# A decoder layer on one core: the output norm's reciprocal root as exponential of minus half a logarithm on ScalarE

## What is computed

```python
D_MODEL, SEQ = 1024, 256
def rms_norm(x, g):
    y = x * lax.rsqrt(jnp.mean(x * x, axis=-1, keepdims=True) + 1e-6)
    return y * g
...
h = rms_norm(x, norm_pre_g)
proj = h @ w_in                       # q, k, v, gate of both groups, forget logits
y_a = merge_heads(fox_attention(q_a, k_a, v_a, log_f)) * silu(g_a)
y_b = merge_heads(moba_attention(q_b, k_b, v_b, slopes)) * silu(g_b)
y = concatenate([y_a, y_b]) @ w_out
return x + rms_norm(y, norm_post_g)   # this last norm is what the change touches
```

## Time and profile before

| | |
|---|---|
| median of 3 runs | 152.05 us (150.95 to 152.28) |
| profiled execution, its own time | 150.72 us |
| span of its instructions | 148.9 us |
| TensorE busy | 140.1 us (94%) |
| VectorE, ScalarE, GpSimd busy | 114.1, 97.4, 53.2 us |
| mean granted TensorE clock | 0.993 of full speed |

### The profile page before, as it was taken

The page is one execution under the profiler, slowest core; times in us unless marked ns, Lnnn a source line. Parts: engine busy times, 40 slices in busy tenths (PEclk is TensorE's granted clock), DMA queues, the critical chain, the costliest instruction groups (busy, mean ns, idle before and its releaser), DMA issues.

```text
span 148.9 us, 2929 instructions
## 1 busy us (share of the span) xinstructions
PE 140.1 (94%) x1012; PEld 131.1 (88%) x1012; DVE 114.1 (77%) x241; ACT 97.4 (65%) x200; POOL 53.2 (36%) x76
## 2 busy tenths in 40 slices
PE   7899999999999999999999979999999999999930
PEld 7898999999999999999999879899999778898830
DVE  0486956999999996879798897989979796222591
ACT  5467889299954687794995729667676765234340
POOL 5641100000000260077390963919184664120421
PEclk9999999999999999999999999999999999999997
DMA  3899997679676998848654624446460440000034
GB/s 99 241 322 399 399 394 274 226 267 292 259 230 263 405 340 319 258 181 228 178 167 145 211 50 158 151 145 211 141 205 6 150 203 0 0 4 0 0 141 141
DMA packets 13948, 29.05 MB, mean 195 GB/s; under 512 B 1512, under 2 KB 6640, under 8 KB 13680
## 3 DMA queue, kind: packets, MB, share of 16 engines
q1 hardware_dynamic: 13344, 27.66, 54.8%
q10 hardware_dynamic: 592, 1.22, 2.1%
HBM read 25.73 MB, written 1.06 MB: 180 GB/s over the span
## 4 chain that ended last, share of the span: by engine, by line
PE 67%; issue 12%; POOL 11%; DMA 2%; ACT 2%; DVE 2%; POOLq 1%; SPq 0%; DVEq 0%
PE bank L843 30%; PE bank L853 16%; PE bank L1001 11%; POOL bias L321 4%; PE bank L954 4%; POOL probs L338 3%; POOL xg_lo L344 2%; DMA raw<-in_w_units 2%; ACT probs L482 1%; PE bank L935 1%; PE bank L937 1%; PE bank L936 1%; PE bank L943 1%; POOL x_t L373 1%; PE bank L945 1%
## 5 line engine op out<-in xcount | busy, mean ns | idle before, releaser
L574 DVE TENSOR_TENSOR w_lo<-raw,w_hi 128x1024 fp32r<-128x1024 f32 (+1 forms) x34 | 48.3, 1425 | 5.2 <-ACT w_hi L387 5.0
L387 ACT ACTIVATE w_hi<-raw 128x1024 fp32r<-128x1024 f32 (+1 forms) x34 | 35.7, 1060 | 6.8 <-PE bank L843 2.8
L843 PE MATMUL bank<-h_lo,w_hi 128*128 128x256 f32 x128 | 35.6, 278 | 0.0
L843 PE MATMUL bank<-h_hi,w_hi 128*128 128x256 f32 x128 | 35.6, 278 | 0.0
L843 PE MATMUL bank<-h_hi,w_lo 128*128 128x256 f32 x128 | 35.6, 278 | 0.0
L321 POOL TENSOR_TENSOR bias<-squares,causal 128x256 f32<-128x256 f32 (+1 forms) x8 | 12.5, 1587 | 35.1 <-DMA squares<-decay_rows_scratch 35.1
L338 POOL TENSOR_TENSOR probs<-probs,row_inv 128x256 f32<-128x256 f32 (+1 forms) x16 | 12.9, 827 | 33.7 <-DVE row_inv L716 33.7
L843 PEld LDWEIGHTS bank<-h_hi,w_hi 128*128 128x128 f32 x128 | 24.1, 188 | 0.5
L843 PEld LDWEIGHTS bank<-h_lo,w_hi 128*128 128x128 f32 x128 | 24.0, 188 | 0.5
L843 PEld LDWEIGHTS bank<-h_hi,w_lo 128*128 128x128 f32 x128 | 24.0, 188 | 0.0
L482 ACT ACTIVATE probs<-logits,neg_max 128x128 f32<-128x128 f32 (+1 forms) x32 | 14.2, 445 | 12.4 <-DVE neg_max L710 12.4
(11 more groups left out here) (123 smaller groups left out, 311.2 us busy)
## 6 DMA issues: line engine op xcount, KB each, us to landing
raw<-in_w_units SPq DMA_DIRECT2D x30, 512.0 KB, 5.5
raw_out<-in_w_out SPq DMA_DIRECT2D x4, 512.0 KB, 6.6
v_pair<-v SPq DMA_DIRECT2D x8, 256.0 KB, 4.1
raw<-in_w_out SPq DMA_DIRECT2D x4, 512.0 KB, 3.5
h<-in_x SPq DMA_DIRECT2D x2, 512.0 KB, 7.6
squares<-decay_rows_scratch ACTq DMA_DIRECT2D x1, 1024.0 KB, 5.7
x_t<-in_x SPq DMA_DIRECT2D x1, 1024.0 KB, 5.1
raw<-in_w_units SPq DMA_DIRECT2D x3, 256.0 KB, 4.7
```

What stands on the lines that cost most here:

```text
L387: nc.scalar.activation(w[0][:, s, 0:width], raw[:, s, 0:width], ACT.Copy).then_inc(s_hi, 1)
L574: nc.vector.tensor_tensor(w[1][:, s, 0:width], raw[:, s, 0:width], w[0][:, s, 0:width].bitcast(F32), ALU.subtract).then_inc(s_lo, 1)
L843: last = nc.tensor.matmul(dst, stationary(a, j), moving(b, j), start=n == 1, stop=n == count * len(PASSES))
```

## The change

For each row tile ScalarE computes rstd itself. VectorE adds up only the groups before the last one, with EPS: that is `ms` now, a partial mean square. ScalarE takes Ln of (last group's sum / 1024 + partial mean square), the partial mean square being the activation's bias, and then Exp of minus half of it, which is `rstd`. The one-element Sqrt ahead of the loop, both roots, the reciprocals and the Newton steps are gone. VectorE multiplies group 1 by the gains right behind group 0's sum, waits for row tile 0's `rstd` behind group 2's product, and adds up groups 2 and 3 ahead of the products of groups 3 and 4.

```diff
--- before.py
+++ after.py
@@ -543,14 +543,16 @@
             probs_high(PAIRS - 1)
             y_high(PAIRS - 1)
 
-            nc.scalar.activation(junk[:, 0, 0:1], rstd[:, 0:1], ACT.Sqrt).then_inc(s_table, 1)
-            act.wait_ge(s_table, 2)
             for n, (t, cols, group) in enumerate(out_groups):
                 act.wait_ge(s_group, n + 1)
                 nc.scalar.activation(junk[:, t, cols], group, ACT.Square, accum_out=out_sq[:, n:n + 1]).then_inc(s_osq, 1)
                 if cols.stop == D_MODEL:
                     act.wait_ge(s_oms, t + 1)
-                    nc.scalar.activation(root[:, t:t + 1], ms[:, t:t + 1], ACT.Sqrt).then_inc(s_oroot, 1)
+                    act.wait_ge(s_osq, n + 1)
+                    nc.scalar.activation(root[:, t:t + 1], out_sq[:, n:n + 1], ACT.Ln, bias=ms[:, t:t + 1],
+                                         scale=1.0 / D_MODEL).then_inc(s_oroot, 1)
+                    act.wait_ge(s_oroot, t + 1)
+                    nc.scalar.activation(rstd[:, t:t + 1], root[:, t:t + 1], ACT.Exp, scale=-0.5).then_inc(s_rstd, 1)
             act.wait_ge(s_ypost, len(out_groups))
             act.wait_ge(s_rstd, TT + 1)
             nc.scalar.activation(y_post[:, 1, HALF + SEQ:], y_post[:, 1, HALF + SEQ:], ACT.Copy,
@@ -791,8 +793,8 @@
                 kept = group if n == 3 else y_post[:, t, cols]
                 nc.vector.tensor_tensor(kept, group, gpost_row[:, cols], ALU.mult).then_inc(s_ypost, 1)
 
-            def out_rstd(t, groups):
-                r, a, m = newton[:, 0, t:t + 1], newton[:, 1, t:t + 1], ms[:, t:t + 1]
+            def out_partial(t, groups):
+                m = ms[:, t:t + 1]
                 for n in groups:
                     dve.wait_ge(s_osq, n + 1)
                     if n == groups[0]:
@@ -803,15 +805,6 @@
                     if n != groups[-1]:
                         link(ins)
                 ins.then_inc(s_oms, 1)
-                times_g(groups[-1])
-                dve.wait_ge(s_oms, t + 1)
-                link(nc.vector.tensor_scalar(a, m, -0.5, None, ALU.mult))
-                dve.wait_ge(s_oroot, t + 1)
-                link(nc.vector.reciprocal(r, root[:, t:t + 1]))
-                link(nc.vector.scalar_tensor_tensor(out=a, in0=r, scalar=a, in1=r, op0=ALU.mult, op1=ALU.mult))
-                nc.vector.scalar_tensor_tensor(out=rstd[:, t:t + 1], in0=a, scalar=1.5, in1=r, op0=ALU.add,
-                                               op1=ALU.mult).then_inc(s_rstd, 1)
-                dve.wait_ge(s_rstd, t + 2)
 
             def residual(t, c, groups):
                 dve.wait_ge(s_ypost, groups)
@@ -821,11 +814,15 @@
                                                in1=x_nat[:, t, cols], op0=ALU.mult, op1=ALU.add).then_inc(s_fin[t][c], 1)
 
             times_g(0)
-            out_rstd(0, (0, 1))
+            out_partial(0, (0,))
+            times_g(1)
             times_g(2)
+            dve.wait_ge(s_rstd, 2)
             residual(0, 0, 1)
+            out_partial(1, (2, 3))
             times_g(3)
-            out_rstd(1, (2, 3, 4))
+            times_g(4)
+            dve.wait_ge(s_rstd, 3)
             residual(1, 0, 3)
             residual(1, 1, 4)
 
```

## The result

| kernel | median us (lowest to highest, runs) | ratio to before, 95% interval |
|---|---|---|
| before | 151.54 (150.85 to 152.40, 6) | |
| changed | 153.00 (152.09 to 153.78, 6) | 1.0117 (1.0073 to 1.0160) |

The ratio is worth 0.0117 x 151.54 = +1.8 us; the forecast was +1.87. In absolute terms the forecast of 153.9 us was 0.9 us above the measured 153.00: 0.5 of that is its base, 152.05 us from three runs where these six have 151.54, and the rest is that the two medians lie 1.46 us apart where the ratio says 1.8. The profiled execution of the changed kernel took 152.47 us (before 150.72), its span is 150.7 us (before 148.9).

The account below looks back on a forecast made before the run. The chain of short steps behind the last matmul was taken to bound the end. Row tile 1's terms sum to 3.27 us for 1.40, +1.87 on a median of 152.05: 153.9 us, 1.2% slower, range 152.6 to 154.9.

Parts of the forecast that it names:

- The end hangs on the stretch from the last read-out to the scaling: Tail behind the last matmul: whatever moves ScalarE's scaling at 144.79 moves the end by as much; 1.40 us is replaced.
- Removed load and Sqrt worth nothing: Ahead of the tail's first square, at 133.18 to 134.67: ScalarE idled another 1.36 us there, so removal gains nothing.
- The sum, 3.27 for 1.40 us: Row tile 1, last read-out to scaling: waits, two loads, Ln, Exp and hand-over take 3.27 us, +1.87 us.
- A set for both functions: Rival, tail's Ln and Exp: one set serves both, row tile 1 takes 0.69 us, 151.3 us in all; chance 0.04.
- A load doesn't run ahead: Rival denied here: a tail load runs beside the Ln or ahead of its wait; +0.6, 152.6 us; chance 0.06.
- a switch costs no more than the load: Rival denied here: each table switch in the tail costs 2.02 us in place of 1.29; 156.1 us; chance 0.04.
- The fourth rival: VectorE's partial sum in the tail is late and the Ln waits: +0.2 to +0.6 more, 154.3 us; chance 0.08.
- Row tile 0's loads are hidden with 0.72 us to spare: ScalarE's tail squares: group 2's starts 1.10 us late, but ScalarE is free at 142.20, before group 4 at 142.92.
- The partial sum is in time by 0.5 us: VectorE, row tile 1: residual (0, 0) takes 1.24 us, two sums 0.17 each, done 144.2; Ln can use it at 144.74.
- GpSimd done with row tile 0 at 143.7, its store and VectorE's issued 1 to 1.5 us later: Row tile 0's end: GpSimd gets rstd at about 141.3, needs 2.42 us, is wanted at 147.2; stores well before the last.
- Chances: Whole kernel: slower 0.74, within 1% 0.24, faster 0.02; 0.80 for a loss over 1% if the forecast holds.

Follow-up runs that it names:

- sums ahead: The changed kernel with VectorE's sums of groups 2 and 3 ahead of the residual of row tile 0: ratio 1.0155 to before, stretch 3.28 us.

## Why the prediction was right, step by step

- *The end hangs on the stretch from the last read-out to the scaling, and nothing ahead of it changes.* Right: TensorE released the squares of groups 1 and 4 within 0.1 us of where it did before, and GpSimd's add and the last store followed the scaling as in the earlier trace rows (0.58 and 1.33 us behind it, before 0.59 and 1.34).
- *Removed load and Sqrt worth nothing.* Right: more idle time in their place.
- *The sum, 3.27 for 1.40 us.* Measured 3.28. By terms: own wait for the square 0.07, measured 0.08; loads 1.28 each; Ln 0.30, measured 0.29; Exp 0.20, measured 0.20; hand-over 0.09, measured 0.10. The experiments with 0 to 3 loads show the two loads as the cause and not only as the rows that are long.
- *Rivals.* A set for both functions would have given 0.69 us; it does, 0.72, where it is loaded by hand. The changed kernel loads twice in each row tile. A load doesn't run ahead, and a switch costs no more than the load: in the changed kernel the Exp's load began 0.02 us behind the Ln's end and the Exp 0.01 behind the load's, and in the run with three loads they follow each other and the Ln follows the second by 0.02. With 0 to 3 loads on the path the stretch grew by 1.28, 1.28 and 1.23 us, each step no more than the load's own 1.28. The fourth rival, a partial sum that comes late, stayed 0.42 us away from holding.
- *Row tile 0's loads are hidden with 0.72 us to spare.* Right for ScalarE's squares (0.75), but this was not the narrowest place. *The partial sum is in time by 0.5 us*: it was, by 0.42, yet not for the reason given. I had the residual slowed by GpSimd to 1.24 us, as if that were its own length. But group 2's sum came at 141.72 and not at 141.90, so the residual began at 142.36, 0.07 us ahead of GpSimd's add; it took 0.74, and the delay fell on the add and on the second sum, which took 1.04 us where I had 0.17. The residual 0.5 us too long and the sum 0.9 too short nearly cancelled, which is luck. The cover is row tile 1's own first load, as in the prediction's sum for the Ln; with that load gone the lateness of row tile 0 came through as 0.9 us of stretch, which no term of the prediction had.
- *GpSimd done with row tile 0 at 143.7, its store and VectorE's issued 1 to 1.5 us later.* Both missed without harm: GpSimd was done at 144.22 (2.0 us later than before) and waited 2.94 us for its last add, not 3.5, and VectorE's residual ended at 143.10, 0.35 later than before.
- *Chances.* The loss is over 1% by its middle, and the interval reaches down to 0.7%.

## What to carry to other kernels

A change that swaps one function for two has to be read in the built order: how many loads stand there, and which of them lie behind a wait on the path. Here the change is worth 0.5% with one set for both functions, asked for by name, and costs 1.2% with the four loads of 1.28 us that the build places by itself. Before a step is called hidden, name all the waits that end at that place, and look which of them is covered only by another cost of the same change.

## What the runs showed of the hardware

- A load of the table set took 1.28 us also where the load before it had brought the same set (run with one load per row tile), and loads in a row didn't overlap: 1.28 us from the start of one to the start of the next (run with three on the path).
- VectorE's sum with two SBUF inputs, one element per partition, issued while GpSimd's add of 512 columns ran, was held up until that add ended: 1.04 us (the changed kernel) and 1.17 us (sums ahead) in place of 0.16, ending in each case within 0.02 us of the add. With one tensor input the same sum took 0.21 us beside it. The other way round, GpSimd's add took 1.79 us in place of 1.30 where it was issued 0.07 us behind the start of VectorE's residual. The sum's time followed what was left of the add when it began (1.02 us in the changed kernel, 1.17 in the run with the sums ahead) and not its own length: 0.88 and 1.01 us on top of 0.16. No run shows what in the hardware the two engines share.
